# Decoder trunk, two layers, one core: last expert's weights in halves, and x summed in the accumulator banks of the second layer

## What is computed

```python
for l in range(2):
    x = x + mixer_l(rms_norm(x, norm_mix[l]))          # layer 0: HGRN2 + GLA; layer 1: retention + RG-LRU
    x = x + hier_moe(rms_norm(x, norm_ffn[l]), ...)    # 32 experts, each token uses 2 of them
return rms_norm(x, norm_final)

def hier_moe(h, ...):                                  # per expert e: w1, w3 are 1024x512, w2 is 512x1024
    hid = silu(xt @ w1e) * (xt @ w3e)
    out += gate[:, e] * (hid @ w2e)

def rms_norm(x, w):
    return x * rsqrt(mean(x * x, axis=-1) + 1e-6) * w
```

## Time and profile before

| | us |
|---|---|
| median of 3 runs | 1203.23 (1202.84 to 1204.14) |
| profiled execution, its own time | 1196.82 |
| span of the profile, first to last instruction | 1195.0 |
| PE / DVE / ACT busy | 882.9 / 348.6 / 303.2 |
| bytes read | 441 MB, 370 GB/s over the span |

### The profile page before, as it was taken

The page is one execution under the profiler, slowest core; times in us unless marked ns, Lnnn a source line. Parts: engine busy times, 40 slices in busy tenths (PEclk is TensorE's granted clock), DMA queues, the critical chain, the costliest instruction groups (busy, mean ns, idle before and its releaser), DMA issues.

```text
span 1195.0 us, 25057 instructions
## 1 busy us (share of the span) xinstructions
PE 882.9 (74%) x10181; PEld 539.1 (45%) x10186; DVE 348.6 (29%) x837; ACT 303.2 (25%) x512; POOL 13.2 (1%) x17
## 2 busy tenths in 40 slices
PE   8999697776666666667669998777666666666664
PEld 6988563443333333333338885334333333333332
DVE  5698562111111111111116884111111111111112
ACT  5644442121011111012014754112110110111102
POOL 2000000000000000000001000000000000000000
PEclk9999899999989989889899999999898888899898
DMA  9634197999999999999996378999999999999994
GB/s 340 242 131 175 55 396 321 429 429 428 428 428 428 429 429 429 428 428 428 429 411 239 142 308 343 376 428 429 427 429 428 429 428 428 428 427 430 429 427 200
DMA packets 44818, 442.69 MB, mean 370 GB/s; under 512 B 3616, under 2 KB 4784, under 8 KB 20080
## 3 DMA queue, kind: packets, MB, share of 16 engines
q1 hardware_dynamic: 44368, 440.90, 88.5%
q10 hardware_dynamic: 288, 1.05, 0.2%
q0 software_dynamic: 128, 0.26, 0.1%
HBM read 441.15 MB, written 1.05 MB: 370 GB/s over the span
## 4 chain that ended last, share of the span: by engine, by line
DMA 51%; PE 36%; DVE 7%; ACT 3%; issue 2%; SPq 1%; DVEq 0%; ACTq 0%
DMA weights<-in_moe_w_dram 51%; PE bank L948 12%; PE bank L590 5%; PE bank L591 5%; PE bank L592 5%; PE bank L957 3%; PE bank L966 2%; PE bank L932 1%; PE bank L755 1%; DVE w_lo L1324 1%; PE bank L784 1%; PE bank L673 1%; ACT w_hi L1059 1%; PE bank L941 1%; DVE gates L1709 1%
## 5 line engine op out<-in xcount | busy, mean ns | idle before, releaser
L948 PE MATMUL bank<-weights,gates 128*32 128x256 f32 x4096 | 289.3, 445 | 136.2 <-DMA weights<-in_moe_w_dram 126.6
L948 PEld LDWEIGHTS bank<-weights,gates 128*32 128x32 f32 x4096 | 148.3, 127 | 261.6 <-DMA weights<-in_moe_w_dram 125.5
L957 PE MATMUL bank<-weights,gates 128*32 128x256 f32 x2048 | 123.8, 382 | 85.9 <-DVE gates L1715 59.3
L1713 DVE TENSOR_TENSOR gates<-gates,bank 128x128 f32<-128x128 f32 x64 | 18.4, 288 | 420.0 <-ACT gates L1001 420.0
L957 PEld LDWEIGHTS bank<-weights,gates 128*32 128x32 f32 x2048 | 62.9, 109 | 146.8 <-issue 85.2
L1001 ACT ACTIVATE gates<-bank 128x128 f32<-128x128 f32 (+1 forms) x68 | 20.0, 296 | 415.2 <-PE bank L948 413.2
L1709 DVE TENSOR_TENSOR gates<-bank,vecs 128x256 f32<-128x256 f32 x64 | 27.2, 425 | 266.2 <-PE bank L941 266.2
L966 PE MATMUL bank<-gates 32*128 32x256 f32 x1024 | 73.3, 400 | 31.2 <-ACT gates L1221 31.2
L1324 DVE TENSOR_TENSOR w_lo<-weights,w_hi 128x2048 fp32r<-128x2048 f32 (+1 forms) x32 | 72.4, 2261 | 32.8 <-ACT w_hi L1059 32.8
L932 PE MATMUL bank<-tok,gates 128*32 128x256 f32 x1024 | 68.5, 385 | 15.7 <-issue 9.9
L966 PEld LDWEIGHTS bank<-gates 32*128 32x128 f32 x1024 | 46.2, 184 | 63.4 <-ACT gates L1221 62.0
(11 more groups left out here) (218 smaller groups left out, 940.0 us busy)
## 6 DMA issues: line engine op xcount, KB each, us to landing
weights<-in_moe_w_dram SPq DMA_DIRECT2D x192, 2048.0 KB, 35.2
weights<-in_even_w_in_dram SPq DMA_DIRECT2D x6, 2048.0 KB, 14.6
weights<-in_odd_w_in_dram SPq DMA_DIRECT2D x5, 2048.0 KB, 21.7
weights<-in_even_w_in_dram SPq DMA_DIRECT2D x2, 1024.0 KB, 9.7
weights<-in_even_w_out_dram SPq DMA_DIRECT2D x1, 2048.0 KB, 7.5
weights<-in_even_w_out_dram SPq DMA_DIRECT2D x2, 1024.0 KB, 4.9
weights<-in_odd_w_out_dram SPq DMA_DIRECT2D x1, 2048.0 KB, 7.4
weights<-in_odd_w_out_dram SPq DMA_DIRECT2D x2, 1024.0 KB, 5.5
```

The costliest lines, as they stand in the source:

```text
L948: ins = pe.matmul(bank[6][PASS * j:PASS * (j + 1), 0:T], got_T[:, k % 2, k // 2, :], up[:, k, :, j * P:(j + 1) * P], start=(k == 0), stop= ...
L957: ins = pe.matmul(bank[7][PASS * q:PASS * (q + 1), T:2 * T], hid_T[:, c, :], down[:, c, q * T:(q + 1) * T], start=(c == 0), stop=(c == Q - 1),
```

## The change

It has three parts.

1. **Halves.** In both layers the last expert (31) is loaded by `last_expert`: w1, w3 and w2 each as two transfers of 1 MiB (8 KB per partition), first halves of w1 and w3, then second halves, then w2's halves. The first halves have their own semaphores (`up_begun`, `down_begun`). PE waits for the first halves, runs steps k = 0 to 3 (for w2, c = 0, 1), and then waits for the second. Between `got_scaled` and the up matmuls of this expert PE runs `keep_warm(8, 4)`.
2. **x in the banks.** In layer 1, `route` begins with 8 matmuls of identity by x (float32, 128x256) into banks 0 to 3, and 4 `keep_warm` matmuls instead of 20. The four clearing matmuls go, for layer 1 only. The banks then collect x plus the sum over experts, and the 8 additions after layer 1 go.
3. **Final norm from the banks.** ACT squares four pieces of 128x512 straight from the banks: channels 0 to 511 of both token blocks, then 512 to 1023. DVE multiplies the banks by the final weight in two pieces of 128x2x512: channels 512 to 1023 first, then, when ACT has squared the first half, channels 0 to 511. One DVE operation adds the partial sums and epsilon. SP issues the store of token block 1; ACT that of block 0.

```diff
+        sums_of_x = ctx.enter_context(nc.psum_tensor("sums_of_x", [P, Q, 512], F32))
+        bank = [sums_of_x[:, q, :] for q in range(Q)] + [...]
...
@@ load_experts
-                for e in range(NE // 3 * 3, NE):
+                for e in range(NE // 3 * 3, NE - 1):
                     take_over(l, e, ORDER[e % 3], up_to(e - 3))
+                last_expert(l, NE - 1, ORDER[(NE - 1) % 3], up_to(NE - 4))
+
+            def last_expert(l, e, slot, before):
+                loads = loads_before(slot, l + 1)
+                sp_q.wait_ge(up_loaded[slot], 32 * (loads - 1))
+                sp_q.wait_ge(up_done, before)
+                for half, loaded in enumerate((up_begun.sem, up_loaded[slot])):
+                    part = slice(half * HALF, (half + 1) * HALF)
+                    for w, src in enumerate((moe_w1, moe_w3)):
+                        sp_q.dma_start(up_of(slot, w)[:, part], src[l, e].rearrange("(p k) f -> p (k f)", k=KC)[:, part]
+                                       ).then_inc(loaded, 16)
+                sp_q.wait_ge(down_loaded[slot], 16 * (loads - 1))
+                sp_q.wait_ge(down_done, before)
+                for half, loaded in enumerate((down_begun.sem, down_loaded[slot])):
...
@@ PE, route and experts
+                if l == 1:
+                    for q in range(Q):
+                        for a in range(TT):
+                            pe.matmul(bank[q][:, a * T:(a + 1) * T], ident, x[:, a, q * T:(q + 1) * T],
+                                      start=(a == 0), stop=True, skip_group_check=True)
-                keep_warm(20, 4)
+                keep_warm(4 if l else 20, 4)
...
+                        if last:
+                            keep_warm(8, 4)
+                            pe.wait_ge(*up_begun.at(l, 32))
+                        else:
+                            pe.wait_ge(up_loaded[slot], 32 * loads)
                         for k in range(KC):
+                            if last and k == KC // 2:
+                                pe.wait_ge(up_loaded[slot], 32 * loads)
...
@@ ACT, after the experts of layer 1
-            norm(4)
-            act.wait_ge(weighed, 1)
+            act.activation(spare[:, 2:3], zeros[:, 0:1], ACT.Sqrt)
+            act.wait_ge(scattered, scatters)
+            for h in range(2):
+                if h:
+                    act.wait_ge(weighed, 1)
+                for a in range(TT):
+                    f(tok[:, a, h * 512:(h + 1) * 512].rearrange("p (q t) -> p q t", q=2), x_half(h)[:, a], ACT.Square,
+                      scale=D ** -0.5, accum_out=head_ss[:, 2 * h + a:2 * h + a + 1]).then_inc(squared.sem, 1)
+            norm_root(4)
+            act.wait_ge(weighed, 2)
...
@@ DVE, after the experts of layer 1
-                for a in range(TT):
+                for a in range(TT if l == 0 else 0):
...
+            for h in (1, 0):
+                if h == 0:
+                    dve.wait_ge(*squared.at(4, 2))
+                tt(x[:, :, h * 512:(h + 1) * 512].rearrange("p a (q t) -> p a q t", q=2), x_half(h),
...
+            dve.wait_ge(*squared.at(4, 4))
+            stt(sums[:, :], head_ss[:, 0:2], EPS, head_ss[:, 2:4], ALU.add, ALU.add).then_inc(mean_set.sem, 1)
```

More of the change, by code:

```diff
@@ L144, in sem, with x_half @@
             return ctx.enter_context(nc.semaphore(name))
-        bank = [ctx.enter_context(nc.psum_tensor(f"bank{i}", [P, 512], F32)) for i in range(8)]
+        sums_of_x = ctx.enter_context(nc.psum_tensor("sums_of_x", [P, Q, 512], F32))
+        bank = [sums_of_x[:, q, :] for q in range(Q)] + [
+            ctx.enter_context(nc.psum_tensor(f"bank{i}", [P, 512], F32)) for i in range(Q, 8)]
+        def x_half(h):
+            return sums_of_x[:, 2 * h:2 * h + 2, :].rearrange("p q (a t) -> p a q t", a=TT)
         weights_at = -(-nc.sbuf_base // 32) * 32
@@ L480, in load_experts @@
                         take_over(l, 3 * i + s, ORDER[s], up_to(3 * i + (s - 3)))
-                for e in range(NE // 3 * 3, NE):
+                for e in range(NE // 3 * 3, NE - 1):
                     take_over(l, e, ORDER[e % 3], up_to(e - 3))
+                last_expert(l, NE - 1, ORDER[(NE - 1) % 3], up_to(NE - 4))
[11 more added lines that the diff above has]
+                for half, loaded in enumerate((down_begun.sem, down_loaded[slot])):
+                    part = slice(half * HALF, (half + 1) * HALF)
+                    sp_q.dma_start(weights[:, slot, 2 * PIECE:][:, part], moe_w2[l, e].rearrange("(p c) d -> p (c d)", c=Q)[:, part]
+                                   ).then_inc(loaded, 16)
             C = EVEN_COLS
@@ L538, in _ @@
             load_experts(1)
+            sp_q.wait_ge(final_set_v, 1)
+            sp_q.dma_start(out[0, P:2 * P, :], tok[:, 1, :]).then_inc(out_stored, 16)
         @block.gpsimd
@@ L919, in start @@
                     pe.wait_ge(*normed.at(2 * l + 1, 2))
-                    for q in range(Q):
-                        zero(q)
+                    if l == 0:
+                        for q in range(Q):
+                            zero(q)
                 def expert(e, slot, loads, passes):
+                    last = isinstance(e, int) and e == NE - 1
                     up = weights[:, slot, 0:2 * PIECE].rearrange("p (w k f) -> p k w f", w=2, k=KC)
@@ L953, in body @@
                         pe.wait_ge(hid_turned, n + 1)
-                        pe.wait_ge(down_loaded[slot], 16 * loads)
+                        if last:
+                            pe.wait_ge(*down_begun.at(l, 16))
+                        else:
+                            pe.wait_ge(down_loaded[slot], 16 * loads)
                         for c in range(Q):
+                            if last and c == Q // 2:
+                                pe.wait_ge(down_loaded[slot], 16 * loads)
                             for q in range(Q):
@@ L1223, in expert @@
                     passes(body)
-                over_experts(act, l, expert, lambda: act.wait_ge(*routed.at(l, 2)))
+                return over_experts(act, l, expert, lambda: act.wait_ge(*routed.at(l, 2)))
             norm(0)
@@ L1246, in _ @@
             route(1)
-            experts(1)
-            norm(4)
-            act.wait_ge(weighed, 1)
+            scatters = experts(1)
+            act.activation(spare[:, 2:3], zeros[:, 0:1], ACT.Sqrt)
[8 more added lines that the diff above has]
+            act.wait_ge(weighed, 2)
             act.wait_ge(final_scale, 1)
@@ L1253, in _ @@
             act.dma_start(out[0, 0:P, :], tok[:, 0, :]).then_inc(out_stored, 16)
-            act.wait_ge(final_set_v, 1)
-            act.dma_start(out[0, P:2 * P, :], tok[:, 1, :]).then_inc(out_stored, 16)
             act.wait_ge(out_stored, 32)
```

9 lines of the change are left out of this document (3 added, 6 removed).

## The result

| | before | after |
|---|---|---|
| median of the runs, us | 1203.68 (1202.84 to 1205.31) | 1196.43 (1194.93 to 1197.28) |
| ratio, 95% interval | | 0.9942 (0.992 to 0.9964) |
| profiled execution, its own time | 1196.82 | 1197.28 |
| span of the profile | 1195.0 | 1195.5 |

The change makes the kernel 7.25 us faster, with the interval 4.3 to 9.6 us. The two profiled executions differ by 0.46 us the other way: before's is 6.0 us faster than the fastest of its runs, after's is its slowest. Whoever compares the two totals of the profiles learns nothing about the change; they have to be cut into stages first.

The account below looks back on a forecast made before the run. The prediction took waiting for expert weights to bound the kernel, with gains only at the ends of the streams and after. It summed 1.9 + 0.5 + 0 + 2.1 = 4.5 us, from 1203.23 to 1198.7, range 1196.5 to 1201.3.

Parts of the forecast that it names:

- What bounds the kernel: Whole kernel: engines wait for weights during the experts' streams, so only their start, their end and what follows can gain.
- Halves, layer 1: Layer 1's last expert: up matmuls start on half the weights and keep the full clock; gain 1.9 us.
- Halves, layer 0: Layer 0's last expert: up matmuls already at full clock, down matmuls end earlier; gain 0.5 us.
- clock luck, both slow: Rival: both last experts' up matmuls were on the lower clock before; total gain 6.1 us, 1197.1; chance 0.18.
- The cost of halves: Last expert's loads: 8 KB runs instead of 16 KB land 0.2 us later, inside the slack; cost 0.
- late halves: Rival: 8 KB runs go at the 2 KB rate, landing 1.6 us later; 1200.7; chance 0.18 with banks doing little.
- each transfer pays its fixed part: Rival: three more transfers cost 2.45 us each per last expert; 8.9 us slower, 1212.1; chance 0.05.
- x in the banks: Layer 1's routing: eight matmuls of x take 3.8 us in place of zero matmuls; gain 0.
- The final norm: After layer 1's last scatter: squares and multiplications straight from the banks; gain 2.1 us, bounds 1.7 and 2.5.
- The sum: All terms: 4.5 us; profiled execution 1192.3, timed runs 1198.7, the terms carried over unchanged.

Follow-up runs that it names:

- e10: The changed kernel with w2 of the last expert loaded in one transfer, w1 and w3 still in halves; median 1198.28 us, ratio 0.9963.
- e3: The changed kernel without the eight zero matmuls ahead of the last expert's up matmuls; median 1196.18 us, ratio 0.993.
- e9: The kernel before plus only the eight zero matmuls ahead of each last expert's wait for its up weights; ratio 0.9976.
- e8: The changed kernel without the eight zero matmuls in either layer and without POOL's share of the first step's w_lo; median 1196.80 us, ratio 0.9939.
- e0: The kernel before, unchanged, run and profiled once more as a control; median 1203.06 us, ratio 1.0004.
- e1: The kernel before plus only the halves and the eight zero matmuls in both layers, final norm as before; median 1198.43 us, ratio 0.9948.
- e2: The changed kernel with the last expert loaded whole and without the eight zero matmuls, leaving x in the banks and the final norm; median 1200.49 us, ratio 0.9968.

## Why the prediction was right, and where it was not

**What bounds the kernel: held, and sharper than stated.** The weights' last bytes decide. Take where PE was released by the last transfer of a layer, from the restart on: after, layer 0, 622.50 - 192.50 = 430.0; e10 with w2 whole, 622.73 - 192.77 = 430.0; e3, layer 1, 1182.14 - 752.29 = 429.9; e9 with everything whole, 430.3 and 1184.13 - 754.41 = 429.7. The stream takes 430.0 ± 0.3 us whatever is done to the last expert. What remains is the down matmuls after it, 1.07 with halves or 1.93 without, and 1.70 to the sum (e3: 1182.14 + 1.07 to 1184.91): a floor of 432.8, and of 433.6 before. The lowest stage of all, layer 1 in e8, was 432.50. The first profile of before had layer 0 at 433.76, on its floor, since its clock held. By this the halves themselves can give 0.9 per layer; in the profiled stages all above that is the clock.

**Halves, layer 1 (1.9): right, a little too large.** The mean of the four profiles of e0's paragraph is 435.10, less 433.72 makes 1.4; against e0 alone it is 1.75. Of the 1.85 forecast 1.63 were the clock and the rest the earlier start. The clock came as forecast, 3.66 us instead of 5.29. The earlier start didn't: counted from the restart, the up matmuls started at 1178.59 - 753.37 = 425.2, against 1173.76 - 748.77 = 425.0 before, since got_scaled came 0.4 later, after 5.91 us of up matmuls in expert 30 where before had 5.35. The 0.9 us of slack for w2's second half was enough.

**Halves, layer 0 (0.5): the term that was mis-sized.** Against the profile used it gave 0.98; against the two profiles in which the clock fell (436.01, 435.90) 3.2; against the mean of four 2.05. The step that failed is taking 615.66 + 3.66 as what before does: the up matmuls took 6.09 and 6.06 us in the other pattern. The rival "clock luck, both slow", 6.1 us in all, is what two of the four profiles of before's last experts show; the prediction gave it 0.18 though its own text said that two thirds of the waiting passes were slow. The zeros, costed as a small loss here, hold the clock in the up matmuls of every profile that has them; by e9 they bring 2.9 us in the kernel before. That the halves would be slower without them is seen in one profile of two (e8: 434.28, e3: 433.09). PE stopped between c = 1 and c = 2 for 0.77 us, where none was forecast with 0.6 to spare. The landing was as estimated, 620.5 - 190.5 = 430.0; it was the pass that came earlier, got_scaled at 613.74 - 192.50 = 421.2 after the restart against 613.30 - 190.49 = 422.8 in the profile that the slack was read from, because expert 30's up matmuls took 3.66 us and not 4.97. A slack of 0.6 us between two chains that shift by 1.6 from one execution to the next is none.

**The cost of halves (0): right.** GB/s stays at 427 to 429 to the end, and the last bytes come at 430.0 with halves and without. The Trainium skill (DMA: Bandwidth & Descriptors, section Bandwidth) lists 341 GB/s for 1 MB; by the estimate from it they would have landed 3.7 us later, so the figure doesn't carry over to these queued transfers. The rivals "late halves" and "each transfer pays its fixed part" fall with it.

**x in the banks (0): right.** The rows that answer to the earlier trace rows:

```profile
737.75 3.72 PE L935 MATMUL sums_of_x<-x,consts 128*128 128x256 f32 x16
741.31 1.03 PE L725 MATMUL bank<-zeros 128*128 128x512 bf16 x4
743.14 0.41 PE L941 MATMUL bank<-y_T,consts 128*128 128x32 f32 x2 [0.80 <-DVE y_T L1731]
...
746.91 1.07 PE L966 MATMUL bank<-tok,gates 128*32 128x256 f32 x16 [1.61 <-DVE gates L1755]
```

3.72 us for the eight (3.8 forecast), PE still waits 0.80 for DVE before L941 and 1.61 before the first gather.

**The final norm (2.1): too small by 0.6.** First store at S + 4.00, not 4.55; end at S + 8.41, not 9.0. A square takes 0.58 to 0.60, as taken from the earlier trace rows, but its accumulator is read while the next square runs (1187.72 and 1187.81): the pitch is 0.57, not 0.71, and four squares end 0.55 us earlier. The multiplications took 1.22 from PSUM, as assumed (1.23).

**The sum.** With the means of before's four profiles: 2.05 + 1.4 + 2.7 = 6.1; with layer 0 at the low clock 3.2 + 1.4 + 2.7 = 7.3. Measured 7.25, 4.3 to 9.6, which both fit; how often the clock falls in the timed runs isn't recorded by expert. e1 alone, 4.7 to 7.8 us, lies above the mean's 2.05 + 1.4 and speaks for the second; but its median, 5.7, is 1.1 over 3.2 + 1.4 too, and no stage shows these. That the range nearly holds 7.25 it owes to the rival to which it gave 0.18, and not to its main sum. On the profiled execution 1192.3 was forecast and 1197.28 came, 5.0 more: 2.5 at the start, 3.6 in the mixer, 0.5 in layer 1's experts, less 0.5 in the first stage, 0.5 in layer 0's experts and 0.6 in the tail. The sentence that "the three terms are differences on a chain that those runs have too" was the weak one: the chain was the same, the clock on it wasn't. Two small sums of the prediction are off: "late halves" at the lower bound of the norm comes to 1203.23 - 2.3 = 1200.9, not 1200.7, and the norm's upper bound lowers 1197.1 by 0.4, not 0.6.

**The start stage (27.8 to 33.4).** It is longer for three reasons that the profiles show. In e2, at 33.35, ACT's first cast of weights began at 13.40 us where it was 10.99 in the first profile of before, 2.4 later. POOL's share then took 3.39 us instead of 2.36. And PE, after 4.28 us of idle time that POOL's share ended, ran at 0.50 from 20 to 24 us where before had 1.00.

**What stays open.** Why the first weights land up to 2.8 us apart between executions, which way the clock goes after idle times of 1.5 to 2.8 us, and where the part of e1's gain lies that no profile places.

## What to carry to other kernels

If the profiled execution undercuts the runs by several times their spread, its durations at the places of the edit are suspect: profile the old kernel again, cut both at anchors that all variants have, and only then price the change. Where PE waits long for the last transfer of a stage, a few matmuls on zeros in front of the wait cost two lines and gave 2.9 to 3.3 us here in the kernel before (e9). Halving the last transfer gives half of the matmuls behind it. Once the halves shorten the wait the zeros may no longer pay (e3), so measure one place at a time. Look at the pass before the wait, too: here a faster one only made the wait longer. A second engine that shares an elementwise operation has to be timed against the first one doing it alone.

## What the runs showed of the hardware

- **DVE and POOL on SBUF at once.** Two subtractions of 128x1024 float32, both operands in SBUF, took 1.32 and 4.14 us (DVE, POOL) in one profile and 3.33 to 3.39 and 2.89 to 2.93 in the others; POOL had started 0.6 us earlier in all of them. DVE alone needs 2.29 for twice as much. The Trainium skill (SBUF — State Buffer, section Who interferes with whom) says that a DVE instruction with two inputs in SBUF contends with a POOL instruction that reads SBUF, that the shared port pair is an exclusive lock, and that the order of issue decides who blocks. The durations agree with a lock (one of the two is stretched by about the other's length). The order does not: POOL started first in both patterns, and in one of them DVE ran nearly undisturbed. At the kernel's start, where DVE was 0.05 us ahead, after had DVE 1.23 and POOL 3.39.
- **The clock is not a property of the kernel.** The same 64 records of layer 0's last expert took 3.66 us after a wait of 2.82 in one execution, and 6.09 after 4.07 in the next. In the four profiles counted above no pass was fast after 3.17 us of idle time or more, and none slow after 1.43 or less.
- **Queued transfers of 1 MiB** with 8 KB per partition lose nothing against 2 MiB with 16 KB, in a stream at 428 GB/s.
